# A mixed attention and MoE layer: the output projection in strict column order, the first normalisations and expert choices later

## Time and profile before

| | |
|---|---|
| median of 3 runs | 1728.47 us (1727.82 to 1728.63) |
| the profiled execution | 1727.39 us, span 1725.6 us |
| mean granted TensorE clock | 0.984 |
| busy: PE / DVE / ACT / POOL | 1611.7 / 620.3 / 265.7 / 101.2 us |
| the twelve jobs of the output projection | 569.2 to 751.2 us |
| first matmul of the first pair of experts | 768.11 us |
| HBM read | 584 MB |

### The profile page before, as it was taken

How to read it: one execution, slowest core, us unless ns; L and a number is a source line. 1 busy time by engine, 2 the same in 40 slices (tenths; PEclk the granted TensorE clock), 3 DMA queues, 4 the chain that set the end, 5 groups by cost and what they waited for, 6 DMA issues and landing times.

```text
span 1725.6 us, 18389 instructions
## 1 busy us (share of the span) xinstructions
PE 1611.7 (93%) x6783; PEld 658.2 (38%) x6828; DVE 620.3 (36%) x1333; ACT 265.7 (15%) x709; POOL 101.2 (6%) x190
## 2 busy tenths in 40 slices
PE   5999999999989999999999999999899989988998
PEld 2445545544433444443323332332333233233332
DVE  3113222202237111352444443445444443544444
ACT  2003222101224000011011101101110110111010
POOL 1022100101011000000000000000000000000000
PEclk9999999999999999999999999999999999999999
DMA  9994671755469722289999999999999999999995
GB/s 369 385 345 194 250 279 64 282 210 219 205 240 380 297 98 98 71 337 424 427 429 429 427 429 425 425 427 427 425 428 423 428 426 427 427 426 427 416 428 222
DMA packets 92639, 581.94 MB, mean 337 GB/s; under 512 B 9138, under 2 KB 24306, under 8 KB 55386
## 3 DMA queue, kind: packets, MB, share of 16 engines
q1 hardware_dynamic: 84944, 554.20, 79.0%
q0 software_dynamic: 5920, 22.63, 3.5%
q10 hardware_dynamic: 1728, 4.51, 0.7%
HBM read 584.06 MB, written 7.05 MB: 343 GB/s over the span
## 4 chain that ended last, share of the span: by engine, by line
PE 71%; DMA 15%; DVE 2%; issue 2%; ACT 1%; SPq 0%; ACTq 0%
PE bank L1221 24%; DMA ring<-in_w 15%; PE bank L969 13%; PE bank L1071 10%; PE bank L1131 7%; PE bank L866 3%; PE bank L1253 2%; PE bank L1056 2%; PE bank L1180 2%; PE bank L1268 1%; PE bank L1203 1%; PE bank L1117 1%; PE bank L1031 1%; PE bank L988 1%; PE bank L1039 1%
## 5 line engine op out<-in xcount | busy, mean ns | idle before, releaser
L1221 PE MATMUL bank<-ring,r 128*64 128x512 f32 x1920 | 470.7, 620 | 44.6 <-DMA ring<-in_w 44.6
L1221 PEld LDWEIGHTS bank<-ring,r 128*64 128x64 f32 x1920 | 129.6, 140 | 303.6 <-issue 303.6
L969 PE MATMUL bank<-ring,r 128*128 128x384 f32 (+1 forms) x672 | 241.5, 518 | 0.0
L1914 DVE TENSOR_TENSOR bank<-bank,r 128x512 f32<-128x512 f32 x192 | 134.3, 699 | 279.1 <-PE bank L1131 266.4
L1253 PE MATMUL bank<-ring,mod_row 128*64 128x512 f32 x896 | 195.8, 593 | 8.0 <-ACT mod_row L1467 7.9
L1071 PE MATMUL bank<-ring,r 128*128 128x512 f32 x384 | 169.6, 595 | 0.7 <-issue 0.7
L969 PEld LDWEIGHTS bank<-ring,r 128*128 128x128 f32 x672 | 126.1, 190 | 108.9 <-issue 45.0
L1131 PE MATMUL bank<-r 128*128 128x512 bf16 x495 | 137.6, 382 | 7.2 <-issue 7.2
L1916 DVE TENSOR_TENSOR r<-r,bank 128x512 f32<-128x512 f32 x192 | 131.9, 687 | 6.6
L1253 PEld LDWEIGHTS bank<-ring,mod_row 128*64 128x64 f32 x896 | 75.3, 137 | 118.9 <-issue 108.6
L1071 PEld LDWEIGHTS bank<-ring,r 128*128 128x128 f32 x384 | 71.3, 190 | 82.6 <-issue 82.5
(11 more groups left out here) (268 smaller groups left out, 1186.7 us busy)
## 6 DMA issues: line engine op xcount, KB each, us to landing
ring<-in_w SPq DMA_DIRECT2D x180, 2048.0 KB, 17.4
ring<-in_w_mod SPq DMA_DIRECT2D x96, 1024.0 KB, 13.0
ring<-in_w SPq DMA_DIRECT2D x19, 1024.0 KB, 5.9
ring<-in_w_o SPq DMA_DIRECT2D x16, 1024.0 KB, 12.4
ring<-in_w_in SPq DMA_DIRECT2D x20, 768.0 KB, 6.6
ring<-in_w_in SPq DMA_DIRECT2D x8, 1024.0 KB, 5.3
r<-mod_d POOLq DMA_DIRECT2D x8, 1024.0 KB, 16.2
r<-in_w SPq DMA_DIRECT2D x5, 1024.0 KB, 7.0
```

Source lines behind the costliest of these rows:

```text
L969: mm = pe.matmul(acc[acc_of(a)][:, 0:w], h_t[:, k, t * P:(t + 1) * P], wu[:, j, :], start=(k == 0), stop=(k == KD - 1))
L1221: mm = pe.matmul(ps[64 * c:64 * c + 64, :], xg_t[:, j, 64 * c:64 * c + 64], big_cut(slot_of(u), (8, 512))[:, j % 8, :], start=(j == 0), st ...
L1914: v.tensor_tensor(ps[:, :], ps[:, :], g2b[:, min(t, 1), cols], ALU.mult).then_inc(strip_scaled, 1)
```

## The change

`OUT_ORDER` becomes plainly chunk by chunk. The latest jobs are then (2,2) (3,0) (3,1) (3,2), so a tile is complete at jobs 9, 10 and 11 instead of 8, 9 and 11, and the numbers that `normalised` and `choose` wait for are raised to fit. normalised(0) moves behind job 9, choose(0) and normalised(1) behind job 10, and choose(1), which needs the logits of job 10, moves in front of the last job's residual.

```
-OUT_ORDER = [(0, 0), (0, 1), (0, 2), (1, 0), (1, 1), (1, 2), (2, 0), (2, 1), (3, 0), (3, 1), (2, 2), (3, 2)]
+OUT_ORDER = [(cc, t) for cc in range(4) for t in range(TILES)]
...
-                v.wait_ge(xa_ready, (9, 10, 12)[t])
+                v.wait_ge(xa_ready, (10, 11, 12)[t])
...
-                v.wait_ge(lg_part, (9, 10, 12)[t])
+                v.wait_ge(lg_part, (10, 11, 12)[t])
...
                     n = OUT_ORDER.index((cc, t))
+                    if n == len(OUT_ORDER) - 1:
+                        choose(1)
                     residual(n)
...
-                    elif n == 8:
+                    elif n == 9:
                         normalised(0)
-                    elif n == 9:
+                    elif n == 10:
                         choose(0)
                         normalised(1)
-                    elif n == 10:
-                        choose(1)
```

## The result

| | before | changed |
|---|---|---|
| median (lowest to highest), 6 runs each | 1728.76 us (1727.82 to 1729.71) | 1735.67 us (1733.43 to 1737.74) |
| ratio, 95% interval | | 1.0042 (1.0031 to 1.0052) |
| profiled execution: time, span | 1727.39, 1725.6 | 1737.74, 1735.9 |

The change makes the kernel 6.9 us slower; forecast were 7.2 us and 1735.7. The profiled execution of the changed kernel is its slowest run: 10.3 us over that of before, 2.4 of them from the front of the kernel, which the change does not touch.

A forecast was written before the change was run, and what follows sets the result against it. Bound taken: a serial engine chain before the MoE's weight stream. 4.36 (held residual) + 0.39 + 0.87 + 1.55 (clock) gave +7.2 us on 1727.39, 1734.6; plus 1.08 to the median, 1735.7 us; range 1732.5 to 1737.2.

The forecast's parts named there:

- The relay as what bounds: From 751.18 us VectorE, TensorE and ScalarE hand work on up to the picks; each microsecond added before the last residual delays everything.
- The order of the jobs, the early loads: Output projection jobs dealt anew cost TensorE 0; loads 4 to 7 leaving some 30 us earlier gain 0.
- First normalisations and choose(0) into the gap: VectorE work moved into the 15.1 us gaps between jobs fills 8 us of a gap, cost 0.
- choose(1) in front of the residual: On VectorE, 0.82 us waiting for the eleventh logits plus 3.54 us of instructions delay the last residual: +4.36 us.
- The clock: TensorE at half speed after its 3.7 us hole: turn +0.39, last logits +0.87, pick(0) +1.55 us.
- Nothing is taken in behind the picks: From the picks on everything shifts alike; the MoE cannot absorb the delay, since its load stream starts there.
- The signs: Expected profile marks: residual 4.4 us late, clock near 0.5 within 755 to 765, first MoE matmul about 775 us.
- Clock kept: Rival: rank matmuls break TensorE's hole, clock stays at 2.4 GHz; price 4.36 us, 1732.8 us, chance 0.09.
- Clock back before pick(0): Rival: clock lost but recovered before tile 0's pick; price up to 5.6 us, 1734.1 us, chance 0.09.
- Absorbed: Rival: weight stream bounds the MoE, so TensorE's late start only shortens later waits; price 0, 1728.5 us, chance 0.08.
- faster: Rival: loads 4 to 7 leaving early start the weight stream 9.8 us earlier; 1718.7 us, chance 0.06.
- One slow stretch of 3.2 us: The Trainium skill's rule, half the slow time lost once per wait: 4.36 + 1.6 = 6.0 us, 1734.4 us.

The follow-up runs named there:

- the old order with the late choice: Kernel before, job order kept, only choose(1) made to wait for the eleventh logits and put in front of the last residual: 1736.3 us, ratio 1.0048.
- the loads held: Changed kernel with loads 4 to 7 of the first MoE pair waiting until job 9 is in x1: 1734.56 us, ratio 1.0036.
- the changed kernel's second one: Second profile of the changed kernel, nothing altered, run again on a second chip: 1734.53 us, ratio 1.0037.
- the filled kernel: Changed kernel plus six f32 matmuls on constants into a free bank, in TensorE's two holes before the last turn: 1731.92 us, ratio 1.0025.
- the kernel with the residual first: Changed kernel with choose(1) behind the last residual, and the last turn and logits ahead of tile 1's ranks on TensorE: 1732.19 us, ratio 1.0026.

## Why the prediction was right

- *The relay as what bounds.* Right: whatever was put into it came out at the end in full, in the eight profiles beside that of before.
- *The order of the jobs, the early loads: 0.* Right as far as two runs can tell, the old order with the late choice (1.0048) and the loads held (1.0036).
- *First normalisations and choose(0) into the gap: 0.* The last job still takes 15.1 us (logits calls at 738.28 and 753.38), and normalised(1) ends at 746.4, 8 us before VectorE is wanted again.
- *choose(1) in front of the residual: +4.36.* Measured 4.36 in the profile after, 4.33 as the whole relay where the clock was held.
- *The clock: +2.8 (0.39 + 0.87 + 1.55).* The mechanism is shown by the fills. By size: turn +0.38 (1.13 for 0.75), logits +0.85 (1.93 for 1.08), and pick(0), from its start to what follows it, +2.5 in the profile after (6.39 for 3.90) and +0.9 in the changed kernel's second one (4.78), for the 1.55 forecast. The forecast of the clock's return (764.3, 3.6 us into the pick) lies between the two that were measured.
- *Nothing is taken in behind the picks.* Right, by the last column of the table.
- *The rivals.* Clock kept is what the filled kernel is, 1.0025 for a price of 4.36 us; no profile of the bare wait shows it. Clock back before pick(0) was not seen either. Absorbed and faster fell by the last column of the table and the loads held. One slow stretch of 3.2 us, priced in the prediction at 6.0 us in all, was too short: the two profiles of the changed kernel have 6.4 and 8.0 us, with the clock down for 6.8 and 10.2. That the holes between the short steps made it longer is the prediction's reason and was not tested by itself.
- *The signs.* The first MoE matmul came at 778.5 for about 775, of which 2.4 us are the front's.
- *Luck.* The medians agree to 0.03 us, but the six runs of the changed kernel spread over 4.3 us, and the 7.2 us forecast lies between the relays of two executions, 6.4 and 8.0. The sum was good to 1 us at best.

## What to carry to other kernels

Where engines hand work to each other with nothing beside it, the place of 15 small instructions in one queue can count more than the order of the big jobs, as it did here: keep them out from in front of the instruction whose input is ready. A wait of some microseconds in TensorE's queue can be paid twice, once as the wait (4.36 us here) and once as half speed behind it (2.1 to 3.7 us). Matmuls into a free bank held the clock up here and were worth their lines; they have to end before the wait does. Compare such kernels by the length of the changed stretch in the profiles too, not by medians alone: here the front of the kernel moves by 4 us from run to run on its own.

## What the runs showed of the hardware

- The clock's return took 7.6 us from the start of the last logits in one profile and 4.3 in another of the same kernel, with TensorE in unbroken work in both. At the MoE's holes it had taken 3.2 and 5.7 us.
- Holes of 0.59, 0.70, 1.01 and 0.87 us, close to each other with little work between, lost the clock (0.60 over 755 to 760 in the kernel with the residual first), while four single holes of 2.74 to 2.77 us in the MoE had not. A fifth of 2.76 us, at 992.22 us in the kernel before, had: the 24 matmuls behind it took 6.70 us, where 5.37 is the fast time.
- The same instructions at 285 to 300 us ran at a granted clock of 1.00 in one execution and 0.77 in another, which took 3.0 us more for them.
